# Moving a bias store ahead of a queue of loads, and the latent sums and tanh steps of a two-block kernel to other places in their stage

## The chip, the cores and the metric

The kernel runs on one core of a Trainium2 chip. The metric is the device time of one execution in microseconds. Five engines work side by side and meet only at semaphores: TensorE (PE in the profile, its weight loads PEld), VectorE (DVE), ScalarE (ACT), GpSimd (POOL) and SyncE (SP). Here SP and POOL only issue DMA transfers, which run on 16 DMA engines.

## The reference

Two transformer-like blocks, one behind the other, on 512 tokens of width 1024 (the first puts 16 meta tokens in front: 528), all in fp32. What matters here, cut down:

```
h = h + 0.5 * swiglu(rmsnorm(h), w_gate, w_up, w_down)       # first FFN, hidden 2816
u = rmsnorm(h)
c_q, c_kv, k_rope, g_q, g_k, g_v, ... = split(u @ w_in)      # the stage "w1"
q  = rmsnorm(c_q)  @ w_uq      # 8 heads x (64 plain + 32 rotary) columns, "uq"
kv = rmsnorm(c_kv) @ w_ukv     # "ukv"
qkv = silu(short_conv(concat(g_q, g_k, g_v), conv_w))        # 4 taps per channel
... attention on q, kv; a gated delta rule on qkv; merge; second FFN ...
# second block:
MOD = ada(c)                   # silu(c) @ w_ada: 3072 outputs, on VectorE row by row
logits + rel_bias[bucket(distance), head]                    # needed late, by the second block
```

## The kernel before

**Weights in chunks.** Every large matrix product streams its weights in chunks of up to 1 MB (`STREAM`), numbered through the program, in two buffers `RAW`, slot 0 and slot 1. fp32 precision is made of three fast products: ScalarE rounds a chunk to `WHI` (L1044), VectorE subtracts to get the rest `WLO` (L1404), and TensorE does WHI\*UH, WLO\*UH and WHI\*UL (L477 to L479). A chunk of the first FFN's gate and up product, or of w1, is 96 matmuls of 128x264. `stream` calls each engine's body once per chunk; in the body for chunk n, ScalarE and VectorE first make WHI and WLO of chunk n+1 (`next_hi`, `next_lo`), which need the product of chunk n-1 to be over, and then do their share of chunk n. SP loads chunk n when WLO of chunk n-2 is done.

**First FFN, stage f1u0.** For each chunk VectorE does one row tile of the ada product (L1440, `ada`), then takes the chunk out of the accumulators (L1468, L1470, L1475, L1478, L1480), with ScalarE doing a tanh and a rounding (L1084, L1086) in between. The ada weights come in 24 tiles of 512 KB in two buffers `ADA`. POOL issues them: the first two at once, each later one when its buffer has been used (`ada_used`).

**The bias rows.** Inside chunk 0 TensorE makes a small table of relative biases (L501); VectorE negates it into `REV` (L1458) and POOL later stores it 128 times over to HBM (L457, `rev`, 3 MB in 2048 rows of 1532 bytes). It is read back only in the second block. POOL's instructions run in their written order: all 24 ada tiles, then the wait for the end of w1, then this store.

**Stage w1** (8 chunks, j = 0 to 7). Chunk 0 holds c_q, chunk 1 c_kv and the rotary key, chunks 2 to 7 the conv channels. VectorE takes each chunk out (L1533), multiplies the latents by their factors (L1588, at j = 4), makes `CLO` (L1593, j = 5) and the rotary key (L1598 to L1601, j = 6), and for the conv does, at each j, first the silu of the channels whose tanh is there (L1578), then the 8 taps of two new channels (L1553, L1556). ScalarE does the tanh of conv channels (L1122), for the pair of chunk c in `conv_tanh(c)`. TensorE sums the squares of the latents with a matrix of ones (L551, `latent_sums`), in the middle of chunks 2 and 4, into unused columns of banks 4 to 6.

**uq and ukv.** TensorE makes the rotary tiles 4 to 7, then the plain tiles 0 to 3, each 6 matmuls of 128x512. VectorE reads the rotary ones (L1617, L1618), ScalarE the plain ones (L1156), and the ukv tiles go into banks that these have left. Then the attention of the first block begins.

Of the kernel before, what the change touches and what calls it, by code (L numbers as in the profile page):

```python
# [76 lines left out]
def build(nc, io):  # L77
# [364 lines left out]
    @block.gpsimd  # L442
    def _(pool):
        pool.wait_ge(h_ld[1], 16)
        pool.dma_start(SILUC[:, :], io["c"].partition_broadcast(P)).then_inc(c_ld, 16)
# [26 lines left out]
    def _(pe):  # L472
# [71 lines left out]
        def latent_sums(n, j):  # L544

            pe.wait_ge(c_sq, j // 2 + 1)
            pe.wait_ge(evac, n)
            for b in range(3):
                a = b * T1 // 3
                for k in ((0, 1) if j == 2 else (2,)):  # L550
                    last = mm(PS[:, 4 + b, 320:320 + T1 // 3], ONES, CF[:, k, a:a + T1 // 3],  # L551
                              start=k != 1, stop=k != 0)
            last.then_inc(c_ss, 1)

        def project(v):
            c0, w = NORMS[v]

            def body(n, j, turn, slot, nxt):
# [5 lines left out]
                for k in range(KD):  # L564
# [3 lines left out]
                    if v == 1 and j in (2, 4) and k == 3:  # L568
                        latent_sums(n, j)
# [464 lines left out]
    def _(act):  # L1034
# [103 lines left out]
        def with_conv(n, j, turn, slot, nxt):  # L1138
# [1141 lines left out]
```

## Time and profile before

| | |
|---|---|
| median of 3 runs | 1784.96 us (1784.18 to 1786.4) |
| the profiled execution | 1784.18 us; its span 1782.5 us |
| TensorE matmul busy | 1644.9 us, 92% |
| VectorE, ScalarE, POOL busy | 941.8, 582.5, 18.0 us |
| mean granted TensorE clock | 0.958 of full speed |
| DMA | 145.32 MB, 82 GB/s on average |

A profile row names the engine, the line, the operation, the tile written and the tiles read. The idle time in square brackets stands ahead of the instruction, with what ended it. Times are from the start of the span; a merged row gives the time from the first instruction's start to the last one's end. The granted clock 1.00 is 2.4 GHz, 0.50 is 1.2 GHz.

### The profile page before, as it was taken

How to read it: one execution, taken by the hardware profiler on the slowest of the kernel's cores; microseconds unless marked ns; L12 is line 12 of the kernel's file. 1: busy time of each engine (PE TensorE's matmuls, PEld its weight loads, DVE VectorE, ACT ScalarE, POOL GpSimd, SP SyncE). 2: the span in 40 equal slices, each digit the busy share in tenths (PEclk: the TensorE clock that was granted, in tenths of full speed). 3: DMA queues.
4: the chain of work that ended last, by engine and by line, in shares of the span. 5: the costliest groups of instructions: out<-in, count | busy, mean ns of one | idle time of the engine just before them, and what ended most of it. 6: DMA issues, size and time to landing. Idle time of an engine off the chain costs nothing.

```text
span 1782.5 us, 30619 instructions
## 1 busy us (share of the span) xinstructions
PE 1644.9 (92%) x12851; PEld 1406.4 (79%) x12851; DVE 941.8 (53%) x1434; ACT 582.5 (33%) x842; POOL 18.0 (1%) x35
## 2 busy tenths in 40 slices
PE   6999999999999648989998999999999899969998
PEld 6999999999975428887776878888887677845767
DVE  3664355554686447664434555534555634445872
ACT  5222122323354520215222232212222455216750
POOL 0000000000000000000000000000000000000000
PEclk9999999999998858999999999999999899978999
DMA  6333233323262000001223222232222321230001
GB/s 234 142 134 105 103 142 133 101 99 115 72 113 42 1 0 3 4 4 47 94 82 106 78 88 94 72 123 100 94 72 90 135 94 61 85 118 1 2 16 57
DMA packets 25957, 145.32 MB, mean 82 GB/s; under 512 B 2720, under 2 KB 2992, under 8 KB 15104
## 3 DMA queue, kind: packets, MB, share of 16 engines
q1 hardware_dynamic: 20768, 123.26, 19.5%
q0 software_dynamic: 5088, 20.58, 4.3%
q8 instruction: 79, 1.29, 0.3%
q14 instruction: 22, 0.18, 0.0%
HBM read 138.60 MB, written 5.23 MB: 81 GB/s over the span
## 4 chain that ended last, share of the span: by engine, by line
PE 82%; DVE 10%; ACT 4%; issue 3%; DMA 1%; DVEq 0%; ACTq 0%; SPq 0%
PE PS L477 21%; PE PS L478 21%; PE PS L479 21%; PE PS L692 2%; DVE WLO L1404 2%; PE PS L702 2%; PE PS L727 1%; ACT WHI L1044 1%; PE PS L632 1%; DVE UMB L1849 1%; DVE TTT L1874 1%; PE PS L714 1%; PE PS L741 1%; PE PS L812 1%; PE PS L828 1%
## 5 line engine op out<-in xcount | busy, mean ns | idle before, releaser
L477 PE MATMUL PS<-UH,WHI 128*128 128x264 f32 (+1 forms) x1640 | 548.1, 334 | 28.1 <-DVE WLO L1404 23.9
L478 PE MATMUL PS<-UH,WLO 128*128 128x264 f32 (+1 forms) x1640 | 543.2, 331 | 0.0
L479 PE MATMUL PS<-UL,WHI 128*128 128x264 f32 (+1 forms) x1640 | 541.1, 330 | 0.0
L477 PEld LDWEIGHTS PS<-UH,WHI 128*128 128x128 f32 x1640 | 310.6, 189 | 65.9 <-issue 17.8
L478 PEld LDWEIGHTS PS<-UH,WLO 128*128 128x128 f32 x1640 | 310.5, 189 | 30.8 <-issue 1.9
L479 PEld LDWEIGHTS PS<-UL,WHI 128*128 128x128 f32 x1640 | 310.2, 189 | 30.4
L1404 DVE TENSOR_TENSOR WLO<-RAW,WHI 128x2048 fp32r<-128x2048 f32 (+3 forms) x125 | 253.4, 2027 | 126.2 <-ACT WHI L1044 125.9
L1044 ACT ACTIVATE WHI<-RAW 128x2048 fp32r<-128x2048 f32 (+3 forms) x125 | 212.0, 1696 | 264.2 <-PE PS L479 252.0
L477 PE MATMUL PS<-GH,WHI 128*128 128x264 f32 (+1 forms) x528 | 169.7, 321 | 4.6 <-DVE GL L1480 3.0
L479 PE MATMUL PS<-GL,WHI 128*128 128x264 f32 (+1 forms) x528 | 169.0, 320 | 0.0
L478 PE MATMUL PS<-GH,WLO 128*128 128x264 f32 (+1 forms) x528 | 168.8, 320 | 0.0
L1084 ACT ACTIVATE TANH<-SILU 128x528 f32<-128x528 f32 (+1 forms) x44 | 28.1, 639 | 266.9 <-DVE SILU L1468 266.9
L477 PEld LDWEIGHTS PS<-GH,WHI 128*128 128x128 f32 x528 | 99.1, 188 | 13.4 <-DVE GL L1480 3.4
L479 PEld LDWEIGHTS PS<-GL,WHI 128*128 128x128 f32 x528 | 99.1, 188 | 7.9
L478 PEld LDWEIGHTS PS<-GH,WLO 128*128 128x128 f32 x528 | 99.1, 188 | 7.4
L1468 DVE TENSOR_TENSOR SILU<-PS,RSTD 128x528 f32<-128x528 f32 (+1 forms) x44 | 30.8, 699 | 110.7 <-PE PS L479 110.7
L1487 DVE SCALAR_TENSOR_TENSOR H<-PS,H 128x528 f32<-128x528 f32 (+3 forms) x32 | 22.4, 699 | 116.1 <-PE PS L479 116.1
L1086 ACT ACTIVATE GH<-GF 128x528 f32 (+3 forms) x44 | 28.1, 639 | 101.5 <-DVE GF L1478 101.5
L1480 DVE TENSOR_TENSOR GL<-GF,GH 128x512 f32 (+3 forms) x44 | 30.8, 701 | 39.5 <-ACT GH L1086 39.5
L1221 ACT ACTIVATE PB<-PS,NM 128x256 f32<-128x256 f32 (+3 forms) x96 | 47.2, 502 | 11.9 <-DVE NM L1700 11.5
L1067 ACT ACTIVATE UH<-H,COL 128x528 fp32r<-128x528 f32 (+1 forms) x32 | 22.2, 723 | 86.4 <-DVE H L1487 44.6
L1470 DVE SCALAR_TENSOR_TENSOR SILU<-TANH,SILU 128x528 f32<-128x528 f32 (+1 forms) x44 | 30.8, 701 | 33.2 <-ACT TANH L1084 33.2
(365 smaller groups left out, 2293.9 us busy)
## 6 DMA issues: line engine op xcount, KB each, us to landing
RAW<-in_f1u SPq DMA_DIRECT2D x22, 1024.0 KB, 4.8
RAW<-in_f2u SPq DMA_DIRECT2D x22, 1024.0 KB, 4.8
ADA<-in_ada POOLq DMA_DIRECT2D x24, 512.0 KB, 4.7
RAW<-in_f1d SPq DMA_DIRECT2D x16, 704.0 KB, 4.1
RAW<-in_f2d SPq DMA_DIRECT2D x16, 704.0 KB, 4.1
RAW<-in_wi SPq DMA_DIRECT2D x10, 1024.0 KB, 4.8
RAW<-in_w SPq DMA_DIRECT2D x8, 1024.0 KB, 4.8
RAW<-in_mg SPq DMA_DIRECT2D x8, 1024.0 KB, 4.7
```

The source lines that it names most:

```text
L477: mm(out, WHI[:, slot, c:c + w], hi, start=first, stop=False)
L478: mm(out, WLO[:, slot, c:c + w], hi, start=False, stop=False)
L479: return mm(out, WHI[:, slot, c:c + w], lo, start=False, stop=last)
L692: last = mm(PS[:, 2 * s + p, c:c + m], P2[rows, q, P * x["qi"]:P * (x["qi"] + 1)], P2[rows, 8 + x["b"], a:a + m], start=True, stop=True)
L702: last = nc.tensor.transpose(PS[:, 4 + p, t * P:(t + 1) * P], PB2[:, s, p, t * P:(t + 1) * P], IDENT)
L1044: A(WHI[:, slot, 0:w], RAW[:, slot, 0:w], ACT.Copy).then_inc(hi_rdy, 1)
L1084: A(TANH[:, slot, 0:w], SILU[:, slot, 0:w], ACT.Tanh, scale=0.5).then_inc(tanh_rdy, 1)
L1221: A(PB2[:, s, p, 0:x["w"]], PS[:, 2 * s + p, 0:x["w"]], ACT.Exp, bias=NM2[:, c:c + 1], scale=-1.0, accum_out=RS2[:, c:c + 1]).then_inc(exp ...
L1404: TT(WLO[:, slot, 0:w], RAW[:, slot, 0:w], WHI[:, slot, 0:w].bitcast(f32), ALU.subtract).then_inc(lo_rdy, 1)
L1468: TT(wide(SILU[:, slot, 0:w]), ps[:, 0:b, :], wide(RSTD[:, c0:c0 + w]), ALU.mult).then_inc(gn_rdy, 1)
L1470: STT(SILU[:, slot, 0:w], TANH[:, slot, 0:w], 1.0, SILU[:, slot, 0:w], ALU.add, ALU.mult)\
L1480: TT(GL[:, j, c0:c0 + w], GF[:, slot, 0:w], GH[:, j, c0:c0 + w].bitcast(f32), ALU.subtract).then_inc(gl_rdy, 1)
```

## The change

Four things are moved; no operation is added or removed. (a) REV is made before the body of chunk 0 on VectorE, so ahead of WLO of chunk 1, and POOL stores it as soon as it is there, ahead of ada tiles 2 to 23. Waits for the end of the store stand on VectorE behind the FFN and no longer on ScalarE late in the program. (b) The latent sums are done between chunks, behind chunks 1 and 3, after the wait that the chunk just multiplied has been taken out. (c) `conv_tanh(c)` is done on ScalarE at j = c+1, not at j = c+2. (d) The rotary tiles of uq go into banks 4 to 7 and the plain ones into 0 to 3, so that TensorE waits for the evacuation of w1's last chunk ahead of the first tile, and the waits of the ukv tiles change places.

```
 # POOL
+        pool.wait_ge(rev_rdy, 1)
+        pool.dma_start(io["rev"][:, :, 0:383], REV[:, :].unsqueeze(1).to_broadcast([16, P, 383]))\
+            .then_inc(rev_st, 16)
+        pool.dma_start(io["rev0"].unsqueeze(1), REV[:, 0:1]).then_inc(rev_st, 16)
         with pool.Fori(1, 12) as i:
             for s in range(2):
                 pool.wait_ge(ada_used, 2 * i + s - 1)
                 pool.dma_start(ADA[:, s, :], io["ada"][2 * i + s]).then_inc(ada_ld[s], 16)
-        pool.wait_ge(rev_rdy, 1)
-        pool.wait_ge(mm_done, START["uq"])
-        ... the same two stores
 # TensorE, w1: latent_sums, called at k == 3 of chunks 2 and 4, is gone; instead
             into(n, j, turn, slot, nxt)
+            if j in (1, 3):
+                pe.wait_ge(c_sq, j // 2 + 2)
+                pe.wait_ge(evac, n + 1)
+                for b in range(3):
+                    a = b * T1 // 3
+                    for k in ((0, 1) if j == 1 else (2,)):
+                        last = mm(PS[:, 4 + b, 320:320 + T1 // 3], ONES, CF[:, k, a:a + T1 // 3],
+                                  start=k != 1, stop=k != 0)
+                last.then_inc(c_ss, 1)
 # TensorE, uq and ukv
-        pe.wait_ge(evac, START["uq"] - 1)
+        pe.wait_ge(evac, START["uq"])
         for t in (4, 5, 6, 7, 0, 1, 2, 3):
-            if t == 0:
-                pe.wait_ge(evac, START["uq"])
-                last = mm3(PS[:, (t + 4) % 8, 0:SEQ], 0, ...
+                last = mm3(PS[:, t, 0:SEQ], 0, ...
         for t in range(4):
-            if t == 0:
+            if t < 2:
+                pe.wait_ge(q_act, 4 * t + 4)
+            elif t == 2:
                 pe.wait_ge(rot_rdy, 1)
-            elif t >= 2:
-                pe.wait_ge(q_act, 4 * t - 4)
 # ScalarE, w1
-            if j >= 4:
-                conv_tanh(j - 2)
+            if 3 <= j < 7:
+                conv_tanh(j - 1)
 # ScalarE, before the norm of the second block
-        act.wait_ge(rev_st, 32)
 # VectorE: out of chunk 0's body, to
+        dve.wait_ge(rev_ps, 1)
+        TS(REV[:, :], PS[0:16, 5, 0:383], -1.0, None, ALU.mult).then_inc(rev_rdy, 1)
         ffn(0, 0, T1)
+        dve.wait_ge(rev_st, 32)
```

The POOL queue, whole but for its ends, before. `ada_used` counts the tiles that VectorE has used; `chunk_multiplied` is `mm_done`.

```order
L445 DMA SILUC<-in_c 128x1024 [waits h_loaded_1]
L447 DMA ADA<-in_ada 128x1024 x2
L450 UNCONDITIONAL_BRANCH
L450 ISA
L453 ISA [waits ada_used]
L453 DMA ADA<-in_ada 128x1024
L453 ISA [waits ada_used]
L453 DMA ADA<-in_ada 128x1024
L450 REGISTER_ALU
L450 COMPARE_AND_BRANCH
L457 DMA rev<-REV 2048x1x383 [waits chunk_multiplied,rev_ready]
L459 DMA rev<-REV 16x1
```

And in the changed kernel:

```order
L445 DMA SILUC<-in_c 128x1024 [waits h_loaded_1]
L447 DMA ADA<-in_ada 128x1024 x2
L451 DMA rev<-REV 2048x1x383 [waits rev_ready]
L453 DMA rev<-REV 16x1
L454 UNCONDITIONAL_BRANCH
L454 ISA
L457 ISA [waits ada_used]
L457 DMA ADA<-in_ada 128x1024
L457 ISA [waits ada_used]
L457 DMA ADA<-in_ada 128x1024
```

The two stores now stand in the same queue ahead of the loop that issues ada tiles 2 to 23.

ScalarE in w1, from the factors of the second latent (RK, at j = 4) to the rounding of chunk 7's weights, before. `conv_done` says that VectorE's taps of that channel are over.

```order
L1044 ACTIVATE WHI<-RAW 128x2048 [waits chunk_multiplied,raw_loaded_1]
L1051 ACT_TABLE_LOAD
L1051 ACTIVATE RK<-PS,CST 128x528 [waits latent_summed]
L1052 ACT_TABLE_LOAD
L1052 ACTIVATE RK<-RK 128x528 [waits scalar_chain]
L1122 ACTIVATE CTT<-CT 128x528 [waits conv_done] x2
L1044 ACTIVATE WHI<-RAW 128x2048 [waits chunk_multiplied,raw_loaded_0]
L1136 ACTIVATE CHI<-CF 128x1584 [waits latent_normed]
L1122 ACTIVATE CTT<-CT 128x528 [waits conv_silu,conv_done] x2
L1044 ACTIVATE WHI<-RAW 128x2048 [waits chunk_multiplied,raw_loaded_1]
```

In the changed kernel, from the tanh of the first pair on:

```order
L1116 ACTIVATE CTT<-CT 128x528 [waits conv_done] x2
L1038 ACTIVATE WHI<-RAW 128x2048 [waits chunk_multiplied,raw_loaded_1]
L1045 ACT_TABLE_LOAD
L1045 ACTIVATE RK<-PS,CST 128x528 [waits latent_summed]
L1046 ACT_TABLE_LOAD
L1046 ACTIVATE RK<-RK 128x528 [waits scalar_chain]
L1116 ACTIVATE CTT<-CT 128x528 [waits conv_silu,conv_done] x2
L1038 ACTIVATE WHI<-RAW 128x2048 [waits chunk_multiplied,raw_loaded_0]
L1130 ACTIVATE CHI<-CF 128x1584 [waits latent_normed]
L1116 ACTIVATE CTT<-CT 128x528 [waits conv_silu,conv_done] x2
L1038 ACTIVATE WHI<-RAW 128x2048 [waits chunk_multiplied,raw_loaded_1]
```

The pair of tanh that belongs to a chunk's taps now stands ahead of the rounding of the chunk after next, where before it stood behind it.

TensorE at the first latent sum, before (in the middle of chunk 2):

```order
L479 MATMUL PS<-UL,WHI 128x264
L551 MATMUL PS<-CF,TAB 128x176 [waits chunk_evacuated,latent_squared,normed_lo_ready]
L551 MATMUL PS<-CF,TAB 128x176 x5
L477 MATMUL PS<-UH,WHI 128x264
L478 MATMUL PS<-UH,WLO 128x264
```

and in the changed kernel (between chunks 1 and 2):

```order
L478 MATMUL PS<-UL,WHI 128x264
L577 MATMUL PS<-CF,TAB 128x176 [waits chunk_evacuated,latent_squared]
L577 MATMUL PS<-CF,TAB 128x176 x5
L476 MATMUL PS<-UH,WHI 128x264 [waits normed_lo_ready,chunk_evacuated,weights_lo_ready]
L477 MATMUL PS<-UH,WLO 128x264
```

The six matmuls are the same; `chunk_evacuated` is now the count that includes the chunk which TensorE has just ended.

## Rows read from the trace of the kernel before

**Rows 1.** The page: TensorE's busy line, and the chain that ended last by engine
```profile
PE 1644.9 (92%) x12851; PEld 1406.4 (79%) x12851; DVE 941.8 (53%) x1434; ACT 582.5 (33%) x842; POOL 18.0 (1%) x35
...
PE 82%; DVE 10%; ACT 4%; issue 3%; DMA 1%; DVEq 0%; ACTq 0%; SPq 0%
```

**Rows 2.** Timeline of VectorE, chunks 0 to 3 of f1u0 (start, us, engine, line, operation)
```profile
32.69 0.54 DVE L1458 TENSOR_SCALAR REV<-PS 16x383 f32<-16x383 f32 x1 [8.28 <-PE PS L501]
...
55.92 1.22 DVE L1440 SCALAR_TENSOR_TENSOR JUNK<-ADA,SILUC 128x1024 f32<-128x1024 f32 x1
...
59.04 0.71 DVE L1468 TENSOR_TENSOR SILU<-PS,RSTD 128x528 f32<-128x528 f32 x1 [1.90 <-PE PS L479]
...
65.35 2.29 DVE L1404 TENSOR_TENSOR WLO<-RAW,WHI 128x2048 fp32r<-128x2048 f32 x1 [0.96 <-ACT WHI L1044]
...
70.54 0.71 DVE L1468 TENSOR_TENSOR SILU<-PS,RSTD 128x528 f32<-128x528 f32 x1 [1.76 <-PE PS L479]
```

**Rows 3.** Timeline of POOL: the issue of ada tile 2, and of the store
```profile
38.76 0.53 POOL L453 DMA_DIRECT2D ADA<-in_ada  x1 [25.02 <-DVE JUNK L1440]
...
507.96 1.05 POOL L457 DMA_DIRECT2D rev<-REV  x1 [165.01 <-PE PS L479]
```

**Rows 4.** DMA issues from 507 to 540 us (count, KB each, us to landing)
```profile
rev<-REV POOLq DMA_DIRECT2D x1, 3064.0 KB, 35.5
RAW<-in_z SPq DMA_DIRECT2D x2, 1024.0 KB, 13.9
RAW<-in_mg SPq DMA_DIRECT2D x1, 1024.0 KB, 11.9
rev<-REV POOLq DMA_DIRECT2D x1, 0.1 KB, 35.1
```

**Rows 5.** RAW in 507.5 to 511 us: the two loads' issues, and their landing
```profile
L417 SPq DMA_DIRECT2D RAW<-in_z x2: 328/328/328, 507.7 to 510.1; - x2
...
DMA to landing us min/median/max: 5.5/13.9/22.4
```

**Rows 6.** Timeline of ScalarE: the rounding of chunk 3's weights
```profile
51.67 1.90 ACT L1044 ACTIVATE WHI<-RAW 128x2048 fp32r<-128x2048 f32 x1
```

**Rows 7.** TensorE by stretches: busy, granted clock, DMA share, GB/s
```profile
18.60:24.50 5.90, 5.90 (x50) 1.00 0.97 393
...
978.70:984.60 5.90, 5.90 (x14) 0.50 0.11 46
```

**Rows 8.** Timeline of TensorE: three waits
```profile
156.73 0.40 PE L477 MATMUL PS<-GH,WHI 128*128 128x264 f32 x1 [1.48 <-DVE GL L1480]
...
507.79 0.47 PE L477 MATMUL PS<-CHI,WHI 128*128 128x512 f32 x1 [0.51 <-issue]
...
978.63 0.80 PE L477 MATMUL PS<-MH,WHI 128*128 128x512 f32 x1 [4.28 <-DVE ML L1933]
```

**Rows 9.** Timeline of VectorE in w1, chunks 4 to 7
```profile
472.10 1.32 DVE L1533 TENSOR_TENSOR PR<-PS,KEEP 128x528 f32<-128x528 f32 x2 [4.09 <-PE PS L479]
...
481.49 2.29 DVE L1404 TENSOR_TENSOR WLO<-RAW,WHI 128x2048 fp32r<-128x2048 f32 x1
483.69 1.32 DVE L1533 TENSOR_TENSOR PR<-PS,KEEP 128x528 f32<-128x528 f32 x2
...
492.75 2.28 DVE L1404 TENSOR_TENSOR WLO<-RAW,WHI 128x2048 fp32r<-128x2048 f32 x1
495.73 1.32 DVE L1533 TENSOR_TENSOR PR<-PS,KEEP 128x528 f32<-128x528 f32 x2 [0.70 <-PE PS L479]
...
505.40 2.28 DVE L1404 TENSOR_TENSOR WLO<-RAW,WHI 128x2048 fp32r<-128x2048 f32 x1
```

**Rows 10.** Timeline of ScalarE: a tanh pair in w1, and uq's last plain tile
```profile
480.93 1.32 ACT L1122 ACTIVATE CTT<-CT 128x528 f32<-128x528 f32 x2 [3.90 <-DVE CT L1556]
...
519.16 1.21 ACT L1156 ACTIVATE QH<-PS 64x512 f32<-64x512 f32 x2 [0.17 <-PE PS L479]
```

**Rows 11.** QH: what TensorE waited for at the attention's matmuls (us, times)
```profile
issue: 3.8, 16
```

More of the change, by code:

```diff
@@ L453, in _ @@
                 pool.dma_start(ADA[:, s, :], io["ada"][2 * i + s]).then_inc(ada_ld[s], 16)
-        pool.wait_ge(rev_rdy, 1)
-        pool.wait_ge(mm_done, START["uq"])
-        pool.dma_start(io["rev"][:, :, 0:383], REV[:, :].unsqueeze(1).to_broadcast([16, P, 383]))\
-            .then_inc(rev_st, 16)
-        pool.dma_start(io["rev0"].unsqueeze(1), REV[:, 0:1]).then_inc(rev_st, 16)
         pool.wait_ge(ss_done, TURN[5])
@@ L542, in _ @@
         ffn(0, 0, T1)
[L544 to L553, printed above, removed]
         def project(v):
@@ L567, in body @@
                         square_sums(1)
-                    if v == 1 and j in (2, 4) and k == 3:
-                        latent_sums(n, j)
                     for t in range(2):
@@ L590, in _ @@
         for t in (4, 5, 6, 7, 0, 1, 2, 3):
-            if t == 0:
-                pe.wait_ge(evac, START["uq"])
             for k in range(2):
-                last = mm3(PS[:, (t + 4) % 8, 0:SEQ], 0, (2 * t + k) * P, CHI[:, k, N_META:T1],
+                last = mm3(PS[:, t, 0:SEQ], 0, (2 * t + k) * P, CHI[:, k, N_META:T1],
                            CLO[:, k, N_META:T1], k == 0, k == 1)
@@ L1155, in _ @@
             for p in range(2):
-                A(QH[0:CH, 2 * t + p, :], PS[CH * p:CH * (p + 1), 4 + t, 0:SEQ], ACT.Copy,
+                A(QH[0:CH, 2 * t + p, :], PS[CH * p:CH * (p + 1), t, 0:SEQ], ACT.Copy,
                   scale=scale).then_inc(q_act, 1)
@@ L1456, in up @@
                         if isinstance(q, int) and q == 0:
-                            dve.wait_ge(rev_ps, 1)
-                            TS(REV[:, :], PS[0:16, 5, 0:383], -1.0, None, ALU.mult).then_inc(rev_rdy, 1)
-                        if isinstance(q, int) and q == 0:
                             dve.wait_ge(ct_rdy, 1)
@@ L1616, in _ @@
         for r in range(2):
-            STT(ROT[:, r, :], PS[:, r, 0:SEQ], scale, cos[:, N_META:T1], ALU.mult, ALU.mult)
-            last = STT(ROT[:, 2 + r, :], PS[:, 2 + r, 0:SEQ], scale, sin[:, N_META:T1], ALU.mult, ALU.mult)
+            STT(ROT[:, r, :], PS[:, 4 + r, 0:SEQ], scale, cos[:, N_META:T1], ALU.mult, ALU.mult)
+            last = STT(ROT[:, 2 + r, :], PS[:, 6 + r, 0:SEQ], scale, sin[:, N_META:T1], ALU.mult, ALU.mult)
         last.then_inc(rot_rdy, 1)
```

## The prediction, written before the changed kernel ran

> **What bounds the kernel now.** I read the page first: TensorE is busy for 1644.9 of 1782.5 us, and 82% of the chain that ended last is TensorE [rows 1]. So in most stages an instruction moved on another engine costs nothing until TensorE waits for it, and then it costs its whole wait. Next I read the timelines of the two stages that the diff touches, and the DMA rows, since the diff moves a 3 MB store. In f1u0 a chunk takes 11.5 us (70.54 - 59.04), and VectorE idles for 1.90 us of it [rows 2]: TensorE-bound, with little to spare. In w1 a chunk takes 11.6 us (483.69 - 472.10), and from chunk 5 on VectorE runs without a gap: WLO of chunk 6 (481.49 + 2.29) ends just when chunk 5 does, and then comes that chunk's evacuation [rows 9]. There the two engines are level, so any step that VectorE has to wait for there lengthens the program.
>
> **(a) The store, at POOL.** REV now comes ahead of WLO of chunk 1. VectorE gets it at 32.69 as before, for 0.54 us [rows 2], then makes WLO of chunk 1 until 35.5. TensorE has 24 matmuls of chunk 0 left at 32.6, or 2.9 us at 11.5/96 each, so it asks for that WLO at 35.5: at most 0.2 us, taken as 0. POOL gets REV at 33.2 and issues the store at 33.3, ahead of ada tile 2, which is issued at 38.76 as before [rows 3].
> The store took 35.5 us to land. A 0.1 KB store behind it in POOL's queue took 35.1 us, though it has next to nothing to move [rows 4]: that queue works in order, so tile 2 lands behind the store. The store ends at 33.3 + 35.5 = 68.8. Where it ran before, one 1 MB load ran under it, the other mostly ahead of it [rows 5]; now chunk 3's load is under it (issued at 35.5, when WLO of chunk 1 is done), and some of chunk 4's, issued a chunk later. That adds 0 to 5.5 us (the first z load's whole landing time, taken for an upper end); I take 1.2, about half of its 1 MB at 393 GB/s [rows 7]. Tile 2 itself is 0.52 MB, 1.3 us at that rate. It lands at 71.3.
> VectorE stands at tile 2 from 55.9 [rows 2]; behind it in its order are the evacuation of chunk 2 and WLO of chunk 4, which TensorE needs next but one. From 71.3: ada 1.2 us, then from the start of chunk 2's evacuation to the end of the next WLO 8.6 us (59.04 to 67.64) [rows 2]: 81.1. TensorE starts chunk 4 at 81.2 where it did at 70.5: **+10.7 us**. Bounds: tile 2 landing at 68.8, +8.2; at 68.8 + 5.5 + 1.3 = 75.6, +15.0.
> Chunk 3's load, issued 2.2 us behind the store, is in the place of the second z load, issued 2.1 us behind it, which took 22.4 us against 5.5 for the first [rows 5]. So it lands at 57.9, while ScalarE wants it at 51.67 [rows 6]: WHI to 59.9, WLO to 62.2, chunk 3 runs from 62.2 to 73.8 and not from 58.9. TensorE then waits from 73.8 to 81.2 anyway, so this delay lies inside the 10.7.
> The Trainium skill (DMA: Bandwidth & Descriptors, "Queues, rings and completion order") says that a DMA engine takes turns between its queues, a packet at a time. By turns, a 1 MB load would not be held up for long; the 22.4 us of the row speak against an even split, and the sum goes by the row.
> **Clock.** After a wait of 4.28 us TensorE ran at 0.50, that is at 1.2 GHz, for 5.9 us (978.63); at 0.50 half of the time is lost, 2.95. A wait of 1.48 us (156.73) stands on the other side: I take it that so short a one costs no clock [rows 7, 8]. The wait here is 7.4 us: **+2.8**, bounds 0 and 3.5. Nothing later gives this back: VectorE catches up within a chunk and TensorE is the bound again. First FFN: **+13.5**.
> What the store leaves free is its old time from 508 to 544. The delayed z load isn't waited for there. I take 0; an upper end for a gain is the 3.8 us of "issue" waits at the attention's scores [rows 11].
>
> **(b) Latent sums.** The same matmuls, but TensorE now stands idle until the chunk just made is taken out: 1.32 us of evacuation [rows 9], and by estimate 0.2 us for the last matmul to come out and 0.1 for the semaphore. Twice 1.6: **+3.2**. By the 1.48 us row this costs no clock. The squares they need are made a chunk earlier, so only the evacuation is waited for.
>
> **(c) The tanh order.** ScalarE's pair of tanh needs the taps that VectorE does at the end of its body of chunk j. Before, the rounding of chunk j+2 stood ahead of that pair, now it stands behind: evacuation, taps, tanh, WHI and WLO become one chain. With the rows, from the start of the evacuation of chunk 4 (472.10): the pair ends at 480.93 + 1.32 = 482.25, so +10.15 [rows 9, 10]; WHI 1.9 to +12.1; WLO 2.3 to **+14.4**. The chunk that TensorE does meanwhile is 11.6. Chunk 5's evacuation starts at that +14.4, not at +11.6. Its taps end 9.06 later (492.75 - 483.69), the pair 0.7 behind them, WHI and WLO: +14.1. Chunk 6: taps 9.67 (505.40 - 495.73), and so +14.65. Sum 43.1 from 472.10. At j = 3 the body lacks the latents' three operations (2.1 us) and the silu pair (1.3): 14.4 - 3.4 = 11.0, under the 11.6 of a chunk, so no wait there.
> **(d) uq's first tile** then waits for chunk 7's evacuation too, 1.35: 44.5 in all. Before, TensorE started uq at 507.79 [rows 8], 35.7 behind 472.10. So (c) and (d) together: **+8.7** (some 7.4 of the order, 1.4 of the bank wait). The ukv tile 1 now waits for ScalarE's last copy, over at 519.16 + 1.21 = 520.4 [rows 10]; tile 0, six matmuls, started when that copy did and takes some 0.7 us, and TensorE's own wait for the last uq tile 0.3: about **+0.3**. Ahead of uq TensorE is idle for 4.3 us (chunk 7 is over at 40.1 of those 44.5), like the wait of 4.28 [rows 8]: clock **+2.7**, on the path, as uq's tiles are TensorE-bound. Waits of 2.4 to 2.9 us ahead of chunks 6 and 7 may lower the clock too, but TensorE has that much to spare in each. w1 with uq: 3.2 + 8.7 + 0.3 + 2.7 = **+14.9**. Bounds: (b) alone, 3.2; or with two more clock drops, 19.
>
> **Sum.** 13.5 + 14.9 = 28.4 on the profiled execution's 1784.18: 1812.6 us. That execution is 0.8 us under the median of the runs, so I leave the number there.
>
> **Rivals.**
> A. Tile 2 is not late, only w1 pays: 1784.2 + 14.9 = 1799.1. It needs the store to be over by 55. For it: the 35.5 us were measured beside other loads. Against it: two whole loads are 2.1 MB, 5.3 us at 393 GB/s [rows 7], and the rest is the store's own. The Trainium skill (DMA: Bandwidth & Descriptors, "Anatomy of one DMA") gives for such a transfer about 2 us plus its bytes at 436 GB/s. By that rule an estimate for the store is 9.2 us; the row has four times that. 0.08.
> B. Only the FFN and the plain waits pay, since ScalarE finds the taps ready sooner: 13.5 + 3.2 + 1.9 for the uq and ukv waits: 1802.8. Against it: the rows have ScalarE idle for 3.90 us ahead of the pair, ended by the last tap [rows 10]. 0.10.
> C. Chunk 3's load gets nothing until the store is over. The mg load, issued at 535.2, landed 11.9 us later, behind the store's end [rows 4]. Then it lands at 68.8 + 5.5 = 74.3, WLO of chunk 3 is done at 78.6, chunk 4 starts at 90.2: +19.7 for 10.7, 1821.6. Against it: the z load landed (532.5) before the store (543.5). 0.12.
> D. Faster: the store leaves the attention of the first block, and its "issue" waits of 3.8 us go [rows 11]: 1780.4. It decides only if tile 2 lands by 56 and ScalarE's order costs nothing either, as in A and B together; each cost must fail. 0.03. The same without the gain is no change, 0.03.
>
> **Numbers.** Forecast 0.64, its own range 1806 to 1819. What can be told from no change is about 0.2%, 3.6 us. A and C stand at either end, so the range is 1798 to 1822. Faster 0.03, same 0.03, slower 0.94.
>
> **What would show it.** VectorE's ada row of chunk 2 idle for some 15 us with the ADA load named; an ADA tile that takes over 30 us to land; chunk 4 of f1u0 starting near 81 and at 0.50 clock for 5 to 6 us; TensorE waits ahead of the L577 sums of 1.5 us; in w1 waits of 2.4 to 2.9 us ahead of chunks 6 and 7 that end with WLO, and of 4.3 ahead of uq; everything behind 550 us shifted by one constant. I'm wrong if the store lands much sooner beside nothing but weights, if TensorE never waits at w1's chunks 6 and 7, or if the stages behind take less time than before.

## The result and the profile after

The changed kernel takes 1813.63 us (median of 4 runs, 1809.47 to 1818.8), the kernel before 1785.68 us on the same chip (4 runs, 1784.18 to 1786.83). The ratio is 1.0158 with a 95% interval of 1.013 to 1.0187: **slower, by 23 to 33 us**. The forecast was 1812.6 us, slower at 0.94, range 1798 to 1822. The profiled execution of the changed kernel is one of the longer ones: 1815.76 us, span 1814.1 us.

The page of the changed kernel, TensorE's busy line and the chain that ended last, answers to [rows 1]:

```profile
PE 1657.5 (91%) x12851; PEld 1416.2 (78%) x12851; DVE 942.2 (52%) x1434; ACT 582.5 (32%) x842; POOL 17.9 (1%) x35
...
PE 77%; DVE 11%; ACT 5%; issue 3%; DMA 3%; DVEq 0%; ACTq 0%; SPq 0%; POOLq 0%
PE PS L476 20%; PE PS L477 20%; PE PS L478 20%; DMA ADA<-in_ada 2%; PE PS L686 2%; ACT WHI L1038 2%; DVE WLO L1397 2%; PE PS L696 2%; PE PS L721 1%; PE PS L626 1%; DVE CT L1549 1%; PE PS L708 1%; DVE UMB L1842 1%; DVE TTT L1867 1%; PE PS L806 1%
```

The last line splits the chain by line. TensorE's share of the chain fell from 82 to 77%, DMA's rose from 1 to 3%, and 2% of the whole span is one tile of ada weights. TensorE is busy for 12.6 us more with the same 12851 matmuls, so they ran slower.

**The first FFN.** POOL's timeline: the store stands at 33.88, and ada tile 2 is issued at 39.13 as before [rows 3]:

```profile
33.88 1.05 POOL L451 DMA_DIRECT2D rev<-REV  x1 [19.95 <-DVE REV L1503]
...
39.13 0.56 POOL L457 DMA_DIRECT2D ADA<-in_ada  x1 [3.71 <-DVE JUNK L1433]
```

DMA issues from 30 to 80 us (count, KB each, median us to landing), to be set beside [rows 4]:

```profile
RAW<-in_f1u SPq DMA_DIRECT2D x3, 1024.0 KB, 19.1
rev<-REV POOLq DMA_DIRECT2D x1, 3064.0 KB, 35.7
ADA<-in_ada POOLq DMA_DIRECT2D x3, 512.0 KB, 25.9
rev<-REV POOLq DMA_DIRECT2D x1, 0.1 KB, 35.7
```

The chain of waits from 50 to 90 us (start, us, what) begins with tile 2, in flight from 39.1 to 72.0:

```profile
39.13 32.82 DMA ADA<-in_ada
```

VectorE and ScalarE there, the answer to [rows 2, 6] (time, us, engine, line, then the idle time ahead in brackets with what ended it):

```profile
60.80 2.29 DVE L1397 TENSOR_TENSOR WLO<-RAW,WHI 128x2048 fp32r<-128x2048 f32 x1 [7.95 <-ACT WHI L1038]
72.08 1.23 DVE L1433 SCALAR_TENSOR_TENSOR JUNK<-ADA,SILUC 128x1024 f32<-128x1024 f32 x1 [8.99 <-DMA ADA<-in_ada]
...
79.53 2.29 DVE L1397 TENSOR_TENSOR WLO<-RAW,WHI 128x2048 fp32r<-128x2048 f32 x1 [0.95 <-ACT WHI L1038]
```

```profile
58.76 1.91 ACT L1038 ACTIVATE WHI<-RAW 128x2048 fp32r<-128x2048 f32 x1 [6.64 <-DMA RAW<-in_f1u]
```

VectorE waits twice, once for chunk 3's weights (by way of ScalarE), once for tile 2. These are the waits that TensorE has and did not have before, from 59 to 548 us, each a row of its timeline (the one ahead of uq's L476 at 533.87 answers to 507.79 in [rows 8]):

```profile
63.34 0.36 PE L476 MATMUL PS<-UH,WHI 128*128 128x264 f32 x1 [4.05 <-DVE WLO L1397]
82.07 0.56 PE L476 MATMUL PS<-UH,WHI 128*128 128x264 f32 x1 [5.37 <-DVE WLO L1397]
450.47 0.39 PE L577 MATMUL PS<-CF,TAB 128*128 128x176 f32 x1 [1.50 <-DVE PR L1526]
477.20 0.39 PE L577 MATMUL PS<-CF,TAB 128*128 128x176 f32 x1 [1.51 <-DVE PR L1526]
504.30 0.59 PE L476 MATMUL PS<-UH,WHI 128*128 128x264 f32 x1 [2.78 <-DVE WLO L1397]
518.17 0.39 PE L476 MATMUL PS<-UH,WHI 128*128 128x264 f32 x1 [0.62 <-DVE WLO L1397]
533.87 0.50 PE L476 MATMUL PS<-CHI,WHI 128*128 128x512 f32 x1 [3.82 <-DVE PR L1526]
547.10 0.36 PE L476 MATMUL PS<-CHI,WHI 128*128 128x264 f32 x1 [0.30 <-PE PS L478]
```

Two in the FFN, two ahead of the latent sums, two ahead of w1's chunks 6 and 7, one ahead of uq, one in ukv. The granted clock fell behind the long ones. TensorE by stretches (busy, busy of the weight loads, VectorE, ScalarE, POOL, granted clock, DMA share, GB/s):

```profile
63.40:67.10 3.70, 3.70 (x18) 3.70 (x19) 0.00 (x0) 0.00 (x0) 0.00 (x0) 0.54 1.07 160
80.80:87.50 6.70, 5.43 (x25) 5.46 (x26) 4.99 (x8) 1.53 (x3) 0.53 (x1) 0.50 0.63 230
...
534.70:538.10 3.40, 3.40 (x10) 2.66 (x9) 1.48 (x3) 0.89 (x2) 0.00 (x0) 0.50 1.01 410
...
1640.70:1661.00 20.30, 19.19 (x112) 12.51 (x114) 10.55 (x56) 9.95 (x48) 0.00 (x0) 0.50 0.00 1
```

**Stage w1.** VectorE from chunk 4 on, beside [rows 9], and ScalarE's tanh pairs, beside [rows 10]:

```profile
489.97 1.32 DVE L1526 TENSOR_TENSOR PR<-PS,KEEP 128x528 f32<-128x528 f32 x2 [3.24 <-PE PS L478]
...
501.96 2.29 DVE L1397 TENSOR_TENSOR WLO<-RAW,WHI 128x2048 fp32r<-128x2048 f32 x1 [2.52 <-ACT WHI L1038]
504.16 1.32 DVE L1526 TENSOR_TENSOR PR<-PS,KEEP 128x528 f32<-128x528 f32 x2
...
518.03 1.31 DVE L1526 TENSOR_TENSOR PR<-PS,KEEP 128x528 f32<-128x528 f32 x2
...
532.50 1.31 DVE L1526 TENSOR_TENSOR PR<-PS,KEEP 128x528 f32<-128x528 f32 x2
```

```profile
498.80 1.32 ACT L1116 ACTIVATE CTT<-CT 128x528 f32<-128x528 f32 x2 [10.42 <-DVE CT L1549]
500.02 1.90 ACT L1038 ACTIVATE WHI<-RAW 128x2048 fp32r<-128x2048 f32 x1
```

The chain that the prediction drew is there: the last tap ends ScalarE's wait of 10.42 us, then come the pair, the rounding, VectorE's wait of 2.52 us for it, WLO, and the next evacuation right behind. The evacuations of chunks 4 to 7 now start 14.19, 13.87 and 14.47 us apart, where a chunk's matmuls take 11.6.

Where the shift comes from, by the start of the same instruction in both traces:

| instruction | before | after | shift |
|---|---|---|---|
| evacuation of w1's chunk 0 | 423.03 | 437.42 | 14.4 |
| evacuation of w1's chunk 4 | 472.10 | 489.97 | 17.9 |
| evacuation of w1's chunk 7 | 507.61 | 532.50 | 24.9 |
| first matmul of uq | 507.79 | 533.87 | 26.1 |
| first rotary tile read | 513.71 | 541.38 | 27.7 |
| first softmax of the attention | 528.13 | 556.08 | 27.95 |
| end of the span | 1782.5 | 1814.1 | 31.6 |

0.35 us of the first row is there before anything that was moved: REV itself starts at 32.69 before and at 33.04 after. The shift is 28.0 from the first softmax up to the second block's pair attention at 1600 us, where the last 3.6 us come in: 20.3 us at half clock (last row of the stretches) where the kernel before has 10.2:

```profile
1612.80:1623.00 10.20, 9.06 (x52) 5.90 (x54) 5.08 (x31) 4.85 (x26) 0.00 (x0) 0.50 0.00 0
```

(That is the kernel before.) The experiments below show both lengths, with either order of w1.

### The profile page after: what moved, and what is told of

Read it like the earlier page. It is cut to its first block, busy times and chain, and to the rows that moved or that the text cites. A ratio compares the mean times of both kernels' runs of the same rounds, so it can differ in the third digit from the quotient of the medians.

```text
span 1814.1 us, 30617 instructions
## 1 busy us (share of the span) xinstructions
PE 1657.5 (91%) x12851; PEld 1416.2 (78%) x12851; DVE 942.2 (52%) x1434; ACT 582.5 (32%) x842; POOL 17.9 (1%) x35
## 4 chain that ended last, share of the span: by engine, by line
PE 77%; DVE 11%; ACT 5%; issue 3%; DMA 3%; DVEq 0%; ACTq 0%; SPq 0%; POOLq 0%
PE PS L476 20%; PE PS L477 20%; PE PS L478 20%; DMA ADA<-in_ada 2%; PE PS L686 2%; ACT WHI L1038 2%; DVE WLO L1397 2%; PE PS L696 2%; PE PS L721 1%; PE PS L626 1%; DVE CT L1549 1%; PE PS L708 1%; DVE UMB L1842 1%; DVE TTT L1867 1%; PE PS L806 1%
## 5 line engine op out<-in xcount | busy, mean ns | idle before, releaser
L476 PE MATMUL PS<-UH,WHI 128*128 128x264 f32 (+1 forms) x1640 | 551.1, 336 | 41.0 <-DVE WLO L1397 36.7
L476 PEld LDWEIGHTS PS<-UH,WHI 128*128 128x128 f32 x1640 | 313.3, 191 | 79.3 <-issue 27.6
L476 PE MATMUL PS<-GH,WHI 128*128 128x264 f32 (+1 forms) x528 | 169.7, 321 | 4.6 <-DVE GL L1470 3.0
L476 PEld LDWEIGHTS PS<-GH,WHI 128*128 128x128 f32 x528 | 99.1, 188 | 13.4 <-DVE GL L1470 3.4
L1477 DVE SCALAR_TENSOR_TENSOR H<-PS,H 128x528 f32<-128x528 f32 (+3 forms) x32 | 22.4, 699 | 116.2 <-PE PS L478 116.2
L1215 ACT ACTIVATE PB<-PS,NM 128x256 f32<-128x256 f32 (+3 forms) x96 | 47.2, 501 | 11.5 <-DVE NM L1693 11.1
```

Of the source, the lines that this page charges most:

```text
L476: mm(out, WHI[:, slot, c:c + w], hi, start=first, stop=False)
L1215: A(PB2[:, s, p, 0:x["w"]], PS[:, 2 * s + p, 0:x["w"]], ACT.Exp, bias=NM2[:, c:c + 1], scale=-1.0, accum_out=RS2[:, c:c + 1]).then_inc(exp ...
```

## The experiments

Each edit was made alone first. In every one the start of the first softmax is a good measure of what the edit cost, since the time spent at half clock differs in later stages; before it is at

```profile
528.13 0.38 ACT L1190 ACTIVATE PB<-PS,NM 128x144 f32<-128x144 f32 x1 [0.70 <-DVE NM L1647]
```

The traces do not start alike: REV, which stands ahead of everything that the edits slow down, starts between 31.85 and 33.81 us, and at 32.69 in the kernel before. So the table gives the shift of the first softmax twice, from the start of the span and counted from REV on; the second is what the edit cost. Beside it stand the ratio of the times, to runs of the kernel before on the same chip, and the time spent at half clock from 1578 us on, in the pair attention, in each profiled execution.

| kernel | median us | ratio (95% interval) | first softmax | shift | from REV on | pair attention at 0.50 |
|---|---|---|---|---|---|---|
| changed kernel | 1813.63 | 1.0158 (1.013 to 1.0187) | 556.08 | 28.0 | 27.6 | 47.8 |
| e1: (a) alone | 1799.11 | 1.0084 (1.0057 to 1.011) | 542.42 | 14.3 | 13.9 | 37.5 |
| e2: (b) alone | 1787.93 | 1.002 (1.0008 to 1.0033) | 530.97 | 2.8 | 3.6 | 37.5 |
| e3: (c) alone | 1798.15 | 1.007 (1.0049 to 1.0092) | 539.42 | 11.3 | 11.5 | 37.5 |
| e4: (d) alone | 1786.64 | 1.0009 (0.9997 to 1.0021) | 529.39 | 1.3 | 1.6 | 37.5 |
| e5: (a), store by ScalarE | 1802.3 | 1.0083 (1.0059 to 1.0108) | 543.13 | 15.0 | 15.8 | 37.5 |
| e6: (a), store in 8 pieces | 1785.02 | 0.9991 (0.9978 to 1.0004) | 528.80 | 0.7 | 0.1 | 37.5 |
| e7: REV early, store late | 1786.2 | 0.9996 (0.9983 to 1.001) | 528.92 | 0.8 | 0.1 | 37.5 |
| e8: changed, without (c) | 1808.77 | 1.0115 (1.0083 to 1.0147) | 547.65 | 19.5 | 19.1 | 47.8 |
| e9: (a), tile 2 ahead | 1792.07 | 1.0038 (1.0024 to 1.0052) | 533.59 | 5.5 | 6.1 | 47.8 |
| e10: (a), half of the store | 1789.02 | 1.0015 (1.0004 to 1.0026) | 530.60 | 2.5 | 1.9 | 47.8 |
| e11: (c), store in 8 pieces | 1795.47 | 1.0061 (1.0045 to 1.0078) | 536.36 | 8.2 | 7.1 | 47.8 |
| e12: changed, store in 8 pieces | 1799.08 | 1.0068 (1.0055 to 1.0082) | 542.04 | 13.9 | 13.7 | 47.8 |

### (a) The store

**e1**: edit (a) as in the change, the rest as before.

> The kernel before with edit (a) alone: REV made ahead of chunk 1's WLO, the store ahead of ada tiles 2 to 23. Theory (costs add, each in its own stage): VectorE stands at ada tile 2 for some 9 us, TensorE waits about 4 us ahead of chunk 3 and 5.4 us ahead of chunk 4, the clock is low for 5 to 6 us behind that; w1 starts 14.0 us later than before and the program is 13 to 15 us longer, about 1799. Rival (the store in the FFN is free as long as VectorE is not late elsewhere too; the changed kernel's loss is mainly in w1): under +5 us.

Measured: +14.3 at the first softmax, ratio +0.84% (15 us). TensorE's two waits are those of the changed kernel:

```profile
63.40 0.36 PE L476 MATMUL PS<-UH,WHI 128*128 128x264 f32 x1 [4.07 <-DVE WLO L1402]
82.04 0.56 PE L476 MATMUL PS<-UH,WHI 128*128 128x264 f32 x1 [5.28 <-DVE WLO L1402]
```

So the FFN's share is that of edit (a) alone.

**e7**: REV is made early on VectorE, as in (a), but the store stays at the end of w1.

> The kernel before with REV made ahead of chunk 1's WLO on VectorE, the store left where it was. Theory: 0 to 0.4 us, since that WLO is ready just when chunk 0 ends. Rival (VectorE's late WLO of chunk 1 holds up chunk 1 and the load of chunk 3 issued behind it): +2 us or more, with a wait of TensorE at 35 us.

Measured: no change (0.1 us from REV on). The move of REV on VectorE costs nothing; it is the store's place on POOL that costs.

**e6**: the early store in eight pieces of 256 rows, one ahead of every second ada tile.

```
-        pool.dma_start(io["rev"][:, :, 0:383], REV ... [16, P, 383]))
+        for g in range(8):
+            if g:
+                ... wait for and issue ada tiles 2g and 2g+1
+            pool.dma_start(io["rev"][:, 16 * g:16 * g + 16, 0:383], REV ... [16, 16, 383]))
```

> Edit (a) alone, but the store is cut into 8 pieces of 256 rows, the first ahead of ada tile 2, the others each behind two further tiles. The same bytes and rows in the same stage. Theory: a piece takes about 35.5/8 = 4.4 us, less than the slack of a tile (some 13 us) and of a weight load (11 us): no wait, within 1 us of the kernel before. Rival (each MB stored beside the FFN costs its own DMA time): +10 us or more, spread over the chunks.

Measured: no change from the kernel before (0.1 us from REV on). The same bytes go out in the first FFN. A piece took 6.3 us, not 4.4, and chunk 3's load, issued under the first piece, 7.7 us; both are inside the slack (DMA issues from 30 to 80 us):

```profile
RAW<-in_f1u SPq DMA_DIRECT2D x5, 1024.0 KB, 4.8
ADA<-in_ada POOLq DMA_DIRECT2D x4, 512.0 KB, 5.7
rev<-REV POOLq DMA_DIRECT2D x3, 383.0 KB, 6.3
```

**e5**: the whole store early, but issued from ScalarE's queue, so that it isn't ahead of the ada tiles in POOL's.

> Edit (a) alone, but the same early store is issued from ScalarE's queue, so that ada tile 2 is not behind it in POOL's queue. Theory (the order within POOL's queue makes VectorE stand still; the load on the DMA engines only delays chunk 3's weights): tile 2 lands by 61 us, at the latest 22 us after its issue as chunk 3's load did, the 9 us wait at tile 2 shrinks to under 5 us, the wait ahead of chunk 3 stays near 4 us: +4 to +9 us in all. Rival (the DMA engines' time is what lacks): tile 2 lands at 70 us as before and the program is 13 to 15 us longer.

Measured: +15.0, 15.8 from REV on. It costs more than (a), by another way, so it does not tell the two theories apart as meant. ScalarE is held for 14.79 us in issuing the 2048 rows, and its next operation, the silu that VectorE needs, waits:

```profile
33.15 14.79 ACTq L1077 DMA_DIRECT2D rev<-REV  x1
47.98 1.06 ACT L1080 ACTIVATE SILUT<-SILUC 128x1024 f32<-128x1024 f32 x1 [14.22 <-issue]
```

```profile
60.13 0.56 PE L472 MATMUL PS<-UH,WHI 128*128 128x264 f32 x1 [13.60 <-DVE WLO L1403]
```

Tile 2 was issued only at 52.2, as VectorE was late, took 16.7 us and landed at 68.9, just behind the end of the store (33.15 + 34.8 = 67.95). That fits the theory's 22 us at most and the rival's 70 us alike: a load in another queue than the store's is held back too, and how much of (a)'s cost is POOL's order and how much the DMA engines' time, this run does not show.

The Trainium skill (DMA: Bandwidth & Descriptors, "Issuing engines are not separate DMA queues") says that DMAs of all issuing engines run on the same 16 DMA engines, and that another issuing engine saves only the time of issuing, usually small beside the transfer. The first half agrees: chunk 3's load, issued at 34.8 under this store too, took 19.5 us. The second doesn't: here the issue was 14.8 of 34.8 us, on an engine that others waited for.

**e9**: ada tile 2 ahead of the store on POOL, tile 3 behind it.

```
+        pool.wait_ge(ada_used, 1)
+        pool.dma_start(ADA[:, 0, :], io["ada"][2]).then_inc(ada_ld[0], 16)
         pool.wait_ge(rev_rdy, 1)
         ... the store, then tile 3, then the loop from tile 4 on
```

> Edit (a) alone, but POOL issues ada tile 2 ahead of the store (so the store at about 39 us) and tile 3 on behind it. Theory (what costs is what stands behind the store in POOL's order, and a weight load issued into it): tile 2 lands within 6 us, VectorE doesn't wait at 55.9, and chunk 3's load, issued at 35.5 ahead of the store, lands in time, so neither gap of 4.1 and 5.4 us is there. Tile 3 lands at 38.9 + 35.7 + 1.5 = 76 us, VectorE wants it at about 68, WLO of chunk 5 is done at 76 + 1.2 + 8.6 = 85.8, where TensorE would ask for it at 82: some 4 us of waits in all ahead of chunks 4 and 5, and 1.7 to 3.5 us of clock: +5.5 to +8 us on the kernel before. Rival (the store costs the first FFN its 14 us wherever it stands in it): +13 to +15.

Measured: +5.5 at the first softmax (6.1 from REV on), ratio +0.38% (7 us). The wait ahead of chunk 3 is gone, and tile 2 took 4.0 us. Ahead of chunk 4 TensorE still waits, for 3.15 us in place of 5.28, and now for chunk 4's own load: it was issued 7.7 us behind the store and landed after 22.6 us. VectorE then waits for ada tile 3; TensorE has no wait of over 0.6 us for that one. ScalarE, VectorE and TensorE:

```profile
68.63 1.91 ACT L1047 ACTIVATE WHI<-RAW 128x2048 fp32r<-128x2048 f32 x1 [5.67 <-DMA RAW<-in_f1u]
```

```profile
76.41 1.23 DVE L1442 SCALAR_TENSOR_TENSOR JUNK<-ADA,SILUC 128x1024 f32<-128x1024 f32 x1 [3.54 <-DMA ADA<-in_ada]
```

```profile
73.11 0.56 PE L480 MATMUL PS<-UH,WHI 128*128 128x264 f32 x1 [3.15 <-DVE WLO L1406]
```

Tile 3 landed at 76.3 where 76 was expected. It is what is issued behind the store, on its own queue or another, that is late, not the stage as a whole.

**e10**: only half of the copies early, the other half where the store was.

```
-        pool.dma_start(io["rev"][:, :, 0:383], REV ... [16, P, 383]))
+        pool.dma_start(io["rev"][:, 0:64, 0:383], REV ... [16, 64, 383]))
+        ... and behind the loop, at the end of w1, copies 64 to 127
```

> Edit (a) alone, but only 64 of the 128 copies of REV are stored ahead of the ada tiles; the other 64 are stored at the end of w1. Theory (the store's own length is what counts, some 17 us for a half): it is over at 33.9 + 18 = 52 us, ada tile 2 lands at 53 to 54, ahead of the 55.9 at which VectorE wants it, chunk 3's load lands by 52, and TensorE waits little or not at all: 0 to +2 us on the kernel before. Rival (a load issued right behind the store is held up for about 22 us whatever the store's length): chunk 3's weights land at 58.7 as with the whole store, TensorE waits for 4 us ahead of chunk 3 and loses clock: +5 to +7 us.

Measured: +2.5 at the first softmax (ratio +0.15%, 0.04 to 0.26), and 1.9 from REV on, inside the theory's 0 to +2, though not by its way. The half took 18.7 us, but chunk 3's load took 20.2 us and landed at 56.4, and tile 2 at 58.8, both later than the store's end at 52.8 and than the 52 and 54 expected. So a store shorter by 17.0 us made the load only 2.5 us faster, nearly as the rival had it. It was enough: TensorE's wait shrank from 4.07 to 1.59 us and cost no clock. ScalarE's wait for that load:

```profile
56.51 1.92 ACT L1045 ACTIVATE WHI<-RAW 128x2048 fp32r<-128x2048 f32 x1 [4.18 <-DMA RAW<-in_f1u]
```

How the load is held back can be seen by queue in the changed kernel (packets, MB, share of 16 DMA engines; q0 is POOL's, q1 SP's), from 36 to 51 us:

```profile
q0 software_dynamic: 312, 1.43, 96.8%
q1 hardware_dynamic: 12, 0.10, 1.5%
```

and in e10 from 36 to 50 us:

```profile
q0 software_dynamic: 293, 1.35, 97.5%
```

(q1 has no line there: no packet of it ran.) Chunk 3's load was issued at 36.0 and 36.2, and for some 15 us almost none of its packets ran, whether the store had 19 us more to go or 2. All 16 DMA engines were 97% busy meanwhile, at 1.43 MB in 15 us, 95 GB/s; with loads alone they moved 393 [rows 7]. Why the load starts after 15 us, and not at once or at the store's end, no run here shows.

### (b) and (d): sums and banks

**e2**: the latent sums between the chunks, the rest as before.

> The kernel before with edit (b) alone: latent sums between chunks. Theory: two waits of TensorE of 1.5 us, one evacuation each, +3.4 us, no clock drop at them, nothing else. Rival (VectorE and ScalarE get the factors earlier and give some back in the level part of w1, chunks 5 to 7): 0 to +1.5 us.

Measured: +2.8, and 3.6 from REV on, ratio +0.2%. Two waits of 1.51 us, no drop of the clock, and nothing given back in chunks 5 to 7:

```profile
435.41 0.39 PE L578 MATMUL PS<-CF,TAB 128*128 128x176 f32 x1 [1.51 <-DVE PR L1530]
```

**e4**: the rotary tiles of uq in banks 4 to 7, the rest as before.

> The kernel before with edit (d) alone: uq's tiles in the other banks. Theory: TensorE waits one evacuation of 1.3 us more ahead of uq and 0.3 us ahead of the second ukv tile, no clock drop: +1.6 us. Rival (the wait for the evacuation is hidden behind WLO of uq, which ends last anyway): 0 to +0.3.

Measured: +1.3 at the first softmax, 1.6 from REV on. TensorE waits 1.69 us ahead of uq's first tile, where it waited 0.51 [rows 8]. The interval of the ratio, 1.0009, includes no change; the trace shows what the runs can't tell.

```profile
508.73 0.50 PE L477 MATMUL PS<-CHI,WHI 128*128 128x512 f32 x1 [1.69 <-DVE PR L1531]
```

### (c) The tanh order

**e3**: the order of the tanh alone.

```
-            if j >= 4:
-                conv_tanh(j - 2)
+            if 3 <= j < 7:
+                conv_tanh(j - 1)
```

> The kernel before with edit (c) alone: conv_tanh one body earlier on ScalarE. Theory: taps, tanh, WHI and WLO become one chain of 14.1 to 14.6 us against a chunk of 11.6 us; waits of 2.6, 2 and 3 us ahead of chunks 6, 7 and uq, 7.2 us, plus 0 to 3 us of low clock behind the last: +7 to +10. Rival (the order costs only because the sums and the banks are moved too, since TensorE and VectorE are level here): under +3.

Measured: +11.3 at the first softmax (11.5 from REV on), ratio +0.7% (12.5 us): more than the theory's upper end. The waits in w1 are as expected (2.24, 2.00 and 2.65 us), but then comes one that neither the prediction nor the expectation had:

```profile
539.95 0.61 PE L632 MATMUL PS<-KH,QH 96*128 96x144 f32 x1 [5.38 <-ACT PB L1190]
```

```profile
537.49 1.91 ACT L1044 ACTIVATE WHI<-RAW 128x2048 fp32r<-128x2048 f32 x1 [5.12 <-DMA RAW<-in_z]
```

The store still goes out at the old place here (512.71, when chunk 7 is over), the two z loads are issued behind it, at 514.6 and 517.0, and land after 22.9 and 27.7 us. In the kernel before the first z load was issued 0.3 us ahead of the store and took 5.5 us [rows 5]. SP issues that load when VectorE's last whole WLO of w1 is done, before at 505.40 + 2.28 = 507.7 [rows 9]; the end of chunk 7 on TensorE releases the store, before at 507.96 [rows 3]. With the tanh order that WLO is the late one:

```profile
512.30 2.29 DVE L1404 TENSOR_TENSOR WLO<-RAW,WHI 128x2048 fp32r<-128x2048 f32 x1 [2.52 <-ACT WHI L1044]
```

It ends at 514.6, behind the store's issue, and ScalarE then waits for the load ahead of its first softmax.

**e11**: the same with the store in eight pieces in the FFN, as in e6.

> Edit (c) alone, and the store cut in 8 pieces of 16 copies between the ada tiles of the first FFN, as in the kernel that took the same time as before with that alone. So the store isn't in the way at the end of w1. Theory (5 us of the +12.7 of edit (c) alone were a z load held up behind the store): the waits of 2.0 to 2.7 us ahead of w1's chunks 5 to 7 stay, the wait of 5.4 us at 534 us goes, +7 to +9 us on the kernel before. Rival (the wait of 5.4 us is the tanh order's own): it stays, +12 to +13.

Measured: +8.2 at the first softmax, and the wait of 5.4 us is gone. 1.1 of the 8.2 us were there before REV, which starts at 33.81 here. So the order of the tanh alone costs 7.1 us, at the low end of the theory, and 4.4 us less than in e3. The waits ahead of chunk 6 and uq are 2.25 and 2.65 us; behind the first the clock fell, chunk 6 took longer, and the wait ahead of chunk 7 is 0.50 and not 2.0. The ratio, +0.61% (8 to 14 us), lies mostly above the +7 to +9: of the profiled execution's 11.4 us, 1.1 came before REV and 3.2 behind the first softmax, where the trace has 10.3 us more at half clock in the pair attention than the one of before.

**e8**: the changed kernel with only (c) undone.

> The changed kernel with (c) undone. Theory (additive): the waits ahead of chunks 6, 7 and most of that ahead of uq go, 7.2 us, and the 1.6 us of low clock behind uq's wait: 1.5 to 9 us less than the changed kernel, scores of the first attention starting at 527 + 14 + 3.4 + 1.6 = 546. Rival (with the sums between the chunks, TensorE's waits there gave VectorE room, so that undoing (c) brings less): they start at 549 or later.

Measured: the first softmax at 547.65, between the 546 of the theory and the 549 of the rival, 8.4 us earlier than in the changed kernel (8.5 from REV on). So (c) is worth 8.5 us there, not less than the 7.1 of e11 but 1.4 more, and the rival is out. Ahead of uq TensorE now waits 1.69 us, not 3.82.

### Do they add up?

**e12**: the changed kernel, its store in eight pieces.

> The changed kernel with its store cut in 8 pieces of 16 copies between the ada tiles of the first FFN, all else as changed. Theory (the costs of the first FFN and of w1 add up, and the first is the store's alone): no waits ahead of chunks 3 and 4, w1's waits of 1.5, 1.5, 2.8, 0.6 and 3.8 us stay as in the changed kernel, the first softmax starts at 528.1 + 14 = 542 us, and the time is 14 us under the changed kernel's, at 1799 to 1801 us. The stretch at half clock in the second block's pair attention is 37.5 us long in the kernel before and 47.8 us in the changed one; if that is a matter of the moment it may be either here, 3.7 us apart, if it is the changed order's own it is 47.8 again. Rival (w1's waits were there only since the FFN ended late): the time is within 5 us of the kernel before, 1786 to 1791 us.

Measured: 1799.08 us, first softmax at 542.04: 14.0 us ahead of the changed kernel's, and w1's waits as in it (1.51 twice, 2.78, 0.47 and 3.83 us). The pair attention has 47.8 us at half clock again, which leaves open whether that is the changed order's own; e9 and e10 settle it (below).

```profile
490.25 0.58 PE L481 MATMUL PS<-UH,WHI 128*128 128x264 f32 x1 [2.78 <-DVE WLO L1402]
...
519.82 0.50 PE L481 MATMUL PS<-CHI,WHI 128*128 128x512 f32 x1 [3.83 <-DVE PR L1531]
```

Counted from REV on, (a), (b) and (d) add up: 13.9 (e1), 3.6 (e2) and 1.6 (e4) are 19.1, and e8, which has the three together, measured 19.1. (c) adds 7.1 alone (e11) and 8.5 on top of them. The 1.4 us between are, by their size, what the clock loses behind the wait ahead of uq: with (c) and (d) together that wait is 3.8 us, the clock falls behind it, and from uq's first matmul to the first rotary read 7.5 us pass (541.38 - 533.87); with a wait of 2.65 us (e11) or 1.69 us (e4, e8) it doesn't fall, and 5.9 us pass. That (d) is the partner, and not (a) or (b), is argued from these waits; (c) with (d) alone was not tried. With e3 in place of e11 the parts would sum to 30.6, against 27.6 measured. No version beat the kernel before; e6 equals it.

## Why the prediction was right

**(a), right.** Tile 2 landed at 72.0 (71.3 forecast), chunk 3's load at 58.7 (57.9), chunk 4 started at 82.07 (81.2), and chunk 3 at 63.34 (62.2): each 0.7 to 1.1 us late, of which 0.35 is the late start. Chunk 4 started 11.2 us later than before, that start taken off, where 10.7 was forecast, and ran at 0.50 for 5.43 us (82.07 to 87.50), where 5.9 was: its evacuation came 14.3 us late, so the clock cost 2.8 more, as forecast. In all +14.0 for +13.5.

```profile
82.22 0.71 DVE L1468 TENSOR_TENSOR SILU<-PS,RSTD 128x528 f32<-128x528 f32 x1 [1.93 <-PE PS L479]
96.55 0.71 DVE L1458 TENSOR_TENSOR SILU<-PS,RSTD 128x528 f32<-128x528 f32 x1 [3.92 <-PE PS L478]
```

(Chunk 4's evacuation, before and after.) What the forecast didn't name is a second drop of the clock, behind the 4.05 us ahead of chunk 3: that chunk took 13.36 us and not 11.6. It cost nothing, since TensorE would have waited for chunk 4 anyway; it made that wait 5.37 us and not 7.4. "This delay lies inside the 10.7" holds for it too. One sign was misplaced: VectorE was to idle for some 15 us at tile 2, but it stood 7.95 us at chunk 3's weights first and 8.99 at the tile. Inside the landing time two small errors cancel: the loads made the store 0.2 us longer, where 1.2 was taken, and tile 2 landed 2.4 us behind the store, where 1.3 was.

The two rows by which waits were priced hold at their ends: between full streams of matmuls, 1.48 to 1.69 us cost no clock in the traces shown here, 3.15 us and more did. In between it went either way: behind 2.00 and 2.24 us (e3) and 2.65 us (e3, e11) the granted clock stayed at 1.00, behind 2.25 us (e11) and 2.78 us it fell to 0.50 for 3.4 us.

**The loads under the store, right by analogy.** The landing time of chunk 3's load, 22.7 us, was forecast from one row, the second z load's 22.4 [rows 5]; it held in size, and e10 shows that the number is not set by the store's length. The forecast gave no reason for it beyond the likeness, and none is shown. Rival C, with nothing moved until the store's end, is out: the load landed 10.9 us ahead of it. Rival A is out, and so is D: the scores' waits of "issue", 3.8 us in 16 [rows 11], are unchanged in the changed kernel. By the fit that the Trainium skill gives (DMA: Bandwidth & Descriptors, "Anatomy of one DMA") the estimate for the store was 9.2 us; it took 35.7. That a DMA engine takes turns between its queues, a packet at a time, as the Trainium skill says (DMA: Bandwidth & Descriptors, "Queues, rings and completion order"), doesn't describe the first 15 us either, with 312 packets of one queue to 12 of the other; from 50 to 60 us both queues move, 186 packets to 184.

**(b), right.** 3.2 forecast, 3.5 between the shifts of chunks 0 and 4, 3.6 in e2 from REV on.

**(c) and (d), right.** From chunk 4's evacuation to uq's first matmul 44.5 us were forecast, and 43.9 passed (533.87 - 489.97); before it was 35.7. So +8.2 for +8.7. The evacuations came 14.19, 13.87 and 14.47 us apart for 14.4, 14.1 and 14.65; the forecast's own rows add up to 13.96 and 14.57 for the last two, so a part of that gap is in its sums. The wait ahead of chunk 7, forecast at 2.4 to 2.9 us, was 0.62: the clock had fallen in chunk 6. Rival B is out. What was missed is that (c) alone costs 4.4 us more with the store at its old place (e3, e11). The change as a whole is free of this only because (a) took the store away.

**The clock ahead of uq, mis-sized.** 2.7 was forecast from a stretch of 5.9 us at 0.50; the stretch was 3.4 us (534.70), and the shift between uq's first matmul and the first rotary read is 1.6. This is the one term of the sum that was off by over a third. The drop behind the 2.78 us wait (chunk 6 took 13.25 us, not 11.6) was hidden, as forecast.

**Behind 550 us, half right.** One constant holds up to 1600 us. The 3.6 us in the pair attention were not forecast. Each of the 14 traces has one of two lengths there, 37.5 or 47.8 us at half clock, and e9 and e10, which leave w1 and that stage as they were, have the long one like the changed kernel. So it isn't the changed order of w1. The forecast's base was the profiled execution of before, and its 28.4 us stand against 31.6 between the profiled executions and 27.95 between the medians; that it is nearest to the medians is in part luck, as their interval is 23 to 33 us. What decides the length stays open.

## What to carry to other kernels

Before moving a transfer "out of the way", read how long it took to land and list what is issued behind it, on its own queue and on the others, for that long: here 35.7 us of store made a tile take 32.8 us and a 1 MB load 22.7, where the page of the kernel before has 4.7 and 4.8 as medians. Cutting it into pieces between the loads took the whole cost away (e6). Where two engines are level, an operation moved ahead of the one that feeds the next chunk turns two overlapped chains into one; add up that chain from the rows and compare it with the chunk. And before comparing two traces at a late point, compare them at one ahead of the edit: here up to 1.1 us of a shift was there from the start, as much as some edits cost.

## What was not expected

- A load issued 2 us behind the store got nearly nothing for some 15 us, for a store of 35.7 us and for one of 18.7 us alike. With eight pieces of 6.3 us each, the median load took 4.8 us.
- ScalarE was held for 14.8 us by the issue of one DMA of 2048 rows; POOL's issue of the same store took 1.05 us.
- The cost of (c) hangs on the rest: 11.5 us from REV on with the store at its old place, 7.1 without it, and 8.5 on top of the other three edits.
- Time at half clock in one late stage differs by 10.3 us (some 3.6 us of run time in the changed kernel) between kernels that are alike there.
